# Weight-block sums of w_down made by GpSimd in place of VectorE, in a one-layer decoder trunk

## The reference, cut to what matters

```
gate = jnp.einsum('bsd,df->bsf', h, w_gate[l])
up = jnp.einsum('bsd,df->bsf', h, w_up[l])
x = x + jnp.einsum('bsf,fd->bsd', jax.nn.silu(gate) * up, w_down[l])
return rmsnorm(x, final_norm)
```

## Time and profile before

| | |
|---|---|
| median of three runs | 1979.11 us |
| profiled execution, span | 1977.3 us |
| TensorE matmul busy | 1967.3 us (99%) |
| VectorE busy | 1654.7 us (84%) |
| ScalarE busy | 1126.6 us (57%) |
| GpSimd busy | 167.2 us (8%) |
| granted TensorE clock, mean | 0.999 |

### The profile page before, as it was taken

How to read it: one execution, slowest core, us unless ns; L and a number is a source line. 1 busy time by engine, 2 the same in 40 slices (tenths; PEclk the granted TensorE clock), 3 DMA queues, 4 the chain that set the end, 5 groups by cost and what they waited for, 6 DMA issues and landing times.

```text
span 1977.3 us, 29282 instructions
## 1 busy us (share of the span) xinstructions
PE 1967.3 (99%) x10300; PEld 1691.6 (86%) x10300; DVE 1654.7 (84%) x2386; ACT 1126.6 (57%) x2064; POOL 167.2 (8%) x261
## 2 busy tenths in 40 slices
PE   9999999999999999999999999999999999999998
PEld 7888888888888988888888888888888888888886
DVE  8877767777766999999999999999998688697886
ACT  6566666666346655555646555555556355566643
POOL 5002333223100000000000000000000000000000
PEclk9999999999999999999999999999999999999999
DMA  9322222224334344443434344444347836546433
GB/s 343 127 83 70 70 71 70 69 70 139 102 117 138 119 148 137 130 139 130 137 132 142 131 134 135 136 139 135 132 138 238 303 120 227 176 148 221 126 130 133
DMA packets 132889, 276.16 MB, mean 140 GB/s; under 512 B 13392, under 2 KB 13424, under 8 KB 131744
## 3 DMA queue, kind: packets, MB, share of 16 engines
q1 hardware_dynamic: 120896, 239.65, 37.9%
q0 software_dynamic: 6640, 23.82, 3.1%
q10 hardware_dynamic: 5232, 11.04, 1.6%
HBM read 242.99 MB, written 31.46 MB: 139 GB/s over the span
## 4 chain that ended last, share of the span: by engine, by line
PE 96%; DVE 2%; issue 1%; DMA 1%; ACT 0%; SPq 0%; POOLq 0%; POOL 0%; DVEq 0%; ACTq 0%
PE bank L841 25%; PE bank L844 13%; PE bank L702 7%; PE bank L768 7%; PE bank L770 7%; PE bank L769 7%; PE bank L704 7%; PE bank L703 7%; PE bank L900 3%; PE bank L898 3%; PE bank L899 3%; PE bank L925 2%; PE bank L942 1%; PE bank L910 1%; PE bank L909 1%
## 5 line engine op out<-in xcount | busy, mean ns | idle before, releaser
L841 PE MATMUL bank<-s_two,t_hi 128*128 128x512 f32 x2352 | 557.3, 390 | 0.0
L1485 ACT ACTIVATE t_hi<-t_raw 128x1792 fp32r<-128x1792 f32 x176 | 302.5, 1720 | 358.1 <-DVE t_raw L2155 269.7
L841 PEld LDWEIGHTS bank<-s_two,t_hi 128*128 128x128 f32 x2352 | 433.5, 188 | 84.7
L2161 DVE TENSOR_TENSOR t_lo<-t_raw,t_hi 128x1792 fp32r<-128x1792 f32 x176 | 355.7, 2021 | 20.7 <-ACT t_hi L1485 20.6
L844 PEld LDWEIGHTS bank<-s_two,t_lo 128*128 128x128 f32 x2352 | 298.9, 191 | 10.4 <-DVE t_lo L2161 0.6
L844 PE MATMUL bank<-s_two,t_lo 128*128 128x256 f32 x2352 | 302.1, 283 | 0.4 <-DVE t_lo L2161 0.4
L1136 ACT ACTIVATE w_hi<-raw 128x512 fp32r<-128x512 f32 x268 | 168.8, 631 | 189.5 <-PE bank L770 141.4
L1778 DVE TENSOR_TENSOR w_lo<-raw,w_hi 128x512 fp32r<-128x512 f32 x268 | 184.6, 690 | 56.6 <-ACT w_hi L1136 56.0
L2152 DVE TENSOR_TENSOR t_raw<-t_raw 128x1024 f32<-128x1024 f32 x176 | 215.0, 1221 | 17.2 <-DMA t_raw<-in_w_gu 15.5
L702 PE MATMUL bank<-h_hi,w_hi 128*128 128x512 f32 x416 | 166.0, 399 | 1.1 <-DVE h_lo L1782 0.6
L704 PE MATMUL bank<-h_lo,w_hi 128*128 128x512 f32 x416 | 162.6, 391 | 0.0
(11 more groups left out here) (260 smaller groups left out, 3487.8 us busy)
## 6 DMA issues: line engine op xcount, KB each, us to landing
t_raw<-in_w_gu SPq DMA_DIRECT2D x348, 256.0 KB, 2.8
raw<-in_w_down SPq DMA_DIRECT2D x112, 256.0 KB, 3.6
raw<-in_w_in SPq DMA_DIRECT2D x104, 256.0 KB, 2.7
gu_mid<-part POOLq DMA_DIRECT2D x43, 512.0 KB, 2.9
gu_next<-gu_mid SPq DMA_DIRECT2D x36, 512.0 KB, 6.9
raw<-in_w_out SPq DMA_DIRECT2D x64, 256.0 KB, 3.0
fast_y<-in_w_down SPq DMA_DIRECT2D x24, 512.0 KB, 5.0
fast_z<-in_w_down SPq DMA_DIRECT2D x16, 512.0 KB, 4.7
```

Source lines behind the costliest of these rows:

```text
L841: mm = nc.tensor.matmul(b[:, :], t_hi[r][:, ti, q, :], both, start=d == 0 and q == 0, stop=d == DOUBLES - 1 and q == 1 and i < 4, skip_gro ...
L1485: nc.scalar.activation(t_hi[r][:, :, :, :].rearrange("p a q c -> p (a q c)"), t_raw[r][:, 1:8, :, :].rearrange("p a q c -> p (a q c)"), AC ...
L2161: nc.vector.tensor_tensor(t_lo[r][:, :, :, :].rearrange("p a q c -> p (a q c)"), t_raw[r][:, 1:8, :, :].rearrange("p a q c -> p (a q c)"), ...
```

## The change

`f_sum` moves from VectorE's program to the end of GpSimd's, behind the last `store_gu` and ahead of the four last `invert`. It keeps its operations, operands and semaphores, and all 32 sums are now written one after the other, chunk by chunk, in the order P5, P6, P7, P4, u = 0 before 1. The three calls of `f_sum` go from VectorE's `down_first` and `down`. Two waits for `f_lo_done` are new, since the low half of the buffer's former content must have been taken before GpSimd overwrites it; on VectorE the order of the queue saw to that.

```
-        def f_sum(c, j):                       (VectorE)
...
-                    f_sum(1, s - 26)
...
-                    f_sum(1, 2)
...
-                        f_sum(c2, j2)
...
+        def f_sum(c, j):                       (GpSimd)
+
+            p, u = j // 2, j % 2
+            x, y, z = (fast_raw[b][u][:, :, :].rearrange("p k c -> p (k c)") for b in "xyz")
+            if p == P5:
+                pool.wait_ge(raw_x[u], 16 * c)
+                pool.wait_ge(raw_y[u], 16 * (3 * (c - 1) + 1))
+                nc.gpsimd.tensor_tensor(x, x, y, ALU.subtract).then_inc(f_sum_done, 1)
+            elif p == P6:
+                pool.wait_ge(raw_z[u], 16 * (2 * (c - 1) + 1))
+                pool.wait_ge(f_sum_done, sums_count(c, 2 * P5 + u))
+                pool.wait_ge(f_lo_done, fast_count(c, 2 * P5 + u))
+                nc.gpsimd.tensor_tensor(x, z, x, ALU.subtract).then_inc(f_sum_done, 1)
+            elif p == P7:
+                pool.wait_ge(raw_y[u], 16 * (3 * (c - 1) + 2))
+                nc.gpsimd.tensor_tensor(y, z, y, ALU.subtract).then_inc(f_sum_done, 1)
+            elif p == P4:
+                pool.wait_ge(raw_z[u], 16 * (2 * (c - 1) + 2))
+                pool.wait_ge(f_lo_done, fast_count(c, 2 * P6 + u))
+                nc.gpsimd.tensor_tensor(x, x, z, ALU.subtract).then_inc(f_sum_done, 1)
+
+        for c in range(1, CHUNKS):
+            for p in (P5, P6, P7, P4):
+                for u in range(2):
+                    f_sum(c, 2 * p + u)
```

More of the change, by code:

```diff
@@ L2299, in ahead_down @@
             split(unit // 4, unit % 4)
[L2301 to L2318, removed]
         def a_sums(c, j):
@@ L2620, in _, with f_sum @@
                 invert(3, slice(0, NT))
+        def f_sum(c, j):
+            p, u = j // 2, j % 2
[20 more added lines that the diff above has]
+                    f_sum(c, 2 * p + u)
         for t in range(NT):
```

## The result

The changed kernel took 1996.53 us (median of 4 runs, 1994.62 to 2001.59); the kernel before, run beside it, 1979.24. The ratio is 1.0092, 95% interval 1.0078 to 1.0106: slower by 17.3 us. I had forecast 1988.7, within 1979.0 to 1995.0. The direction and the blocking of VectorE were right; the price of TensorE's waits was not, and the time lies outside the range.

The account below looks back on a forecast made before the run. TensorE alone was taken to bound chunks 1 to 4. Waits of 0.37 us at S13 and 2.8 at P15, together 3.2, at three chunk ends gave 9.6 us: 1979.1 to 1988.7 us, range 1979.0 to 1995.0.

Parts of the forecast that it names:

- What bounds the kernel: Chunks 1 to 4: TensorE alone bounds, busy all 326.50 us; work taken from VectorE can shorten nothing.
- One sum, 2.4 us: A 128x1024 subtraction on GpSimd takes 2.4 us, upper end 2.6, estimated from its 128x512 sums of 1.30 us.
- The block, 2.1 us: Each GpSimd sum meeting a full queue holds up VectorE instructions with two SBUF operands for 2.1 us; 1.14 us is won.
- so it gets its turn after one or two VectorE instructions: GpSimd beside a full VectorE queue waits only that long, read from its 16 scalings of 0.69 to 2.18 us.
- Where the blocks fall: Walk through chunk 2's end: TensorE waits 0.37 us at S13 and 2.8 at P15, likewise ending chunks 1 and 3.
- Sum 5: The next chunk's first P7 sum, expected at a chunk's end before the `w_lo` of P15, the last of three blocks there.
- rival A: GpSimd gets turns late, sum 5 falls behind P15's `w_lo`, each end costs 1.1 us: 1982.4 in all; chance 0.17.
- sum 1: P5, u = 0, end of chunk 2: x lands after 6.2 us, VectorE held 1734.84 to 1736.94, next `gate_scaled` 1.54 us later.
- sum 2: P5, u = 1, end of chunk 2: x issued at 1739.24, `f_lo` of S13 starts at 1745.8 instead of 1743.36.
- Three times 3.2 are 9.6 us: TensorE waits of 3.2 us at each end of chunks 1, 2 and 3, added to the time at their own length.
- Rival B: With a block below 1.4 us, no TensorE wait arises at P15 and time stays at 1979.1; chance 0.19.
- Rival C: More collides: 2.6 us sums give 1991.7; x for sum 1 landing within 5.3 us gives up to 1996; chance 0.14.

Follow-up runs that it names:

- run 5: Kernel before, all sums on VectorE, plus 64 idle GpSimd subtractions of 128x512 at the changed kernel's releases, writing an unread spare buffer: 2000.43 us, ratio 1.0110.
- run 6: Kernel before, plus 160 GpSimd fills (memset) of the spare buffer, five per release, which read nothing from SBUF: 1979.22 us, ratio 1.0001.
- run 3: Changed kernel, but at the ends of chunks 1 to 3 P6's second and P7's first sum wait for the low half of P15: 1983.06 us, ratio 1.0019.
- run 2: Changed kernel with the 8 sums for P7 back on VectorE in their old place, 24 on GpSimd: 1985.67 us, ratio 1.0034.
- run 8: Changed kernel with more sums postponed: P5's behind S13's low half, P6's and P7's first behind P15's, one in chunk 1 behind S2's: 1990.42 us, ratio 1.0056.
- run 4: Kernel before, with 8 extra VectorE additions of 128x512 ahead of the low half of P15 in chunks 1 to 3: 1993.98 us, ratio 1.0075.
- run 7: Kernel before, with 5 extra VectorE additions ahead of the low half of P15 in chunks 1 to 3: 1983.20 us, ratio 1.0022.

## Why the prediction was right in its waits and wrong in their price

**What bounds the kernel: right.** TensorE had no wait to remove, and no run came out faster than the kernel before beyond its interval.

**One sum, 2.4 us: right.** The shortest are 2.39 and 2.40 us.

**The block, 2.1 us: right.** 2.2 us measured, and run 5 shows that it needs no data between the engines, run 6 that it needs GpSimd to read. The Trainium skill, page "SBUF — State Buffer", section "SBUF: two separate sides", has the later instruction stand for the whole of the other, which would give an estimate of 2.4 us; the rows show 2.2, and they decide.

**"so it gets its turn after one or two VectorE instructions": right for 31 of the 32 sums.** The sum at 1608.12 stood for 4.5 us beside six VectorE instructions, the first postponed one at each chunk's end in run 3 for 3.4, and one subtraction of run 5 for 6.5. It happened where it did the forecast no harm; the reading of the 16 scalings was too narrow.

**Where the blocks fall: right at P15, incomplete elsewhere.** "TensorE waits 2.8 us", three times: 3.03, 3.04 and 3.04. Sum 5 came before the `w_lo` of P15 each time, so rival A did not occur there; run 2 shows what it would have given, and run 3 that the two sums concerned make most of the loss. At S13 I had 0.37 each time; it came in chunks 1 and 3 (0.07 and 0.53 of wait, 1.1 us of loss together) and not in chunk 2, from whose rows I had worked it out. There x for sum 1 landed after 8.3 us, not 6.2, so the sum held up `f_lo` of S12 and not `gate_scaled`, x for sum 2 was issued 2 us sooner than in my walk, and sum 2 held up a `gate_times_up` ahead of `f_lo` of S13. The end of the `w_lo` of P15 came out as forecast even so, at 1763.4 of my walk's time; in part that is luck. I had passed over S2 of chunk 1 with "spare time is over 2.2 us and absorbs them": two blocks fell in front of it, 0.7 us. Run 8 failed by the same oversight in a larger form.

**The step that failed: "TensorE waits 0.37", "TensorE waits 2.8 us. Together 3.2 us", "Three times 3.2 are 9.6 us".** I took a wait of TensorE to cost its own length, and put what comes behind it at nothing without a reason. The waits are 10.1 us, close to the 9.6. They cost 17.5, since behind the three long ones the granted clock stood at 0.50 for some 3.2, 5.7 and 2.7 us and the matmuls there started 0.43 us apart in place of 0.23, and since each wait costs some 0.3 us for the pipeline. Runs 4 and 7 isolate this without GpSimd: waits of 0.75 to 1.31 us cost 0.3 more than themselves, waits of 2.9 to 3.45 from 0.3 to 3.0 more. The three long waits cost 2.2 us each over themselves on average (15.7 less 9.1, by three). With this term, taken from the result, the same walk gives 9.6 + 3 x 2.2 = 16.2, and 1995.3, still 1.2 below the measured time. No row of the trace before could have given its size, since TensorE never stood there for over 1.0 us; but it can only add, and my range had no room for it.

**Rival B** (a block below 1.4 us) did not hold: 2.2. **Rival C** came near the time (up to 1996) by a wrong way: a sum with VectorE idle took 2.4 us, not 2.6, and x for sum 1 landed after 6.2, 8.3 and 6.6 us in the three chunks, never within 5.3. **The chances**, 0.67 on slower, stood on the right side. In their sum rival A's share of slower is 0.05, where "0.17, half of it within 0.2%" gives 0.085, and slower would be 0.70. The powers at the end of GpSimd's queue came 66 us after its last sum, not 25, which bears on nothing.

What stays open is which waits bring the clock down. 2.02 us did and 2.54 did not, 2.92 did and 3.42 did not. I have no row that tells the two kinds apart. Open is also when GpSimd's reading instruction holds VectorE up and when VectorE's queue holds GpSimd up.

## What to carry to other kernels

Work moved from VectorE to GpSimd need not leave VectorE: here a GpSimd instruction that reads SBUF mostly held up the next VectorE instruction with two SBUF operands for nearly its whole length (2.2 us for 1.14 taken away), and it did so when its inputs arrived, not where the queue had it. At times it stood itself instead, so its result can be 3 to 7 us late where VectorE's queue is full. Before such a move list the spare time of every low half, for the whole stretch into which a sum can drift, and put each sum behind a wait where a block is covered; if TensorE has no waits, there is nothing to win. And a wait of TensorE of 2 us or more cost up to about twice its length in these runs, one of about 1 us its length and 0.3 us.

## What was not expected of the hardware

TensorE's clock behind waits, over all runs with a wait of 1.9 us or more (the changed kernel, runs 4, 5 and 8): twelve waits, ten of them with matmuls at the lower level behind, and two (3.42 and 2.54 us) without. Behind the ones below 1.4 us the clock stayed. Nor does the fall always come with the first matmul: in the changed kernel it did behind P15's waits in chunks 2 and 3, and came 0.3 us later in chunk 1; in run 8 it came 1.2 and 1.0 us after TensorE had started again at full speed. And GpSimd's fills took 0.53 us each beside a VectorE queue 79% full and stretched nothing, where its subtractions of the same shape went from 1.04 us alone to 1.83 on average.
